# The two row-sum matmuls of the feed-forward input norm, set apart

## What is computed

```python
def rmsnorm(x, g):
    y = x * lax.rsqrt(jnp.mean(x * x, axis=-1, keepdims=True) + EPS)
    return y * g

def swiglu(h, w_gu, w_down):
    gate, up = jnp.split(h @ w_gu, 2, axis=-1)
    return (jax.nn.silu(gate) * up) @ w_down

x = x + swiglu(rmsnorm(x, norm_ffn[i]), ffn_w_gu[i], ffn_w_down[i])
```

## Time and profile before

| | us |
|---|---|
| median of 3 executions | 2921.4 (2918.1 to 2921.99) |
| the profiled execution | 2919.41 |
| its span, first to last instruction | 2917.4 |
| TensorE matmul records, busy | 2848.8 (98%) |
| TensorE weight loads, busy | 2798.8 (96%) |
| GpSimd busy | 2108.9 (72%) |
| ScalarE busy | 1325.1 (45%) |
| VectorE busy | 1074.1 (37%) |

### The profile page before, as it was taken

How to read it: one execution, slowest core, us unless ns; L and a number is a source line. 1 busy time by engine, 2 the same in 40 slices (tenths; PEclk the granted TensorE clock), 3 DMA queues, 4 the chain that set the end, 5 groups by cost and what they waited for, 6 DMA issues and landing times.

```text
span 2917.4 us, 55892 instructions
## 1 busy us (share of the span) xinstructions
PE 2848.8 (98%) x24180; PEld 2798.8 (96%) x24180; DVE 1074.1 (37%) x1883; ACT 1325.1 (45%) x1476; POOL 2108.9 (72%) x462
## 2 busy tenths in 40 slices
PE   8999999999999999999999999999999999999998
PEld 8999889999998899999999998999998999999998
DVE  4317444223165343245333135333134331353331
ACT  5344534344345454345443474543354433454432
POOL 6887558878876578876688783668786588666784
PEclk9999999999999899999999999999999999999999
DMA  8964335555554255554455542445554455544553
GB/s 229 209 209 154 136 124 185 188 186 193 197 180 146 105 201 183 184 180 145 145 188 188 188 175 73 156 163 188 188 189 159 146 187 188 175 155 148 183 185 109
DMA packets 74197, 496.88 MB, mean 170 GB/s; under 512 B 8399, under 2 KB 13135, under 8 KB 14968
## 3 DMA queue, kind: packets, MB, share of 16 engines
q1 hardware_dynamic: 68344, 485.88, 46.5%
q10 hardware_dynamic: 5632, 7.62, 2.5%
HBM read 490.05 MB, written 3.41 MB: 169 GB/s over the span
## 4 chain that ended last, share of the span: by engine, by line
PE 86%; POOL 3%; issue 3%; DVE 3%; DMA 3%; ACT 2%; SPq 0%; POOLq 0%; DVEq 0%; ACTq 0%
PE G L450 21%; PE G L451 21%; PE G L452 21%; PE S L450 6%; PE S L451 6%; PE S L452 6%; POOL wl L399 3%; DMA raw<-w_units 3%; PE G L656 1%; PE S L1006 1%; ACT wh L1077 1%; PE S L531 1%; PE S L805 0%; PE S L768 0%; PE S L762 0%
## 5 line engine op out<-in xcount | busy, mean ns | idle before, releaser
L399 POOL TENSOR_TENSOR wl<-raw,wh 128x2048 fp32r<-128x2048 f32 x458 | 2108.7, 4616 | 778.0 <-ACT wh L1077 757.0
L1077 ACT ACTIVATE wh<-raw 128x2048 fp32r<-128x2048 f32 x456 | 873.0, 1917 | 1086.5 <-DMA raw<-w_units 1086.3
L450 PE MATMUL G<-ah,wl 128*128 128x256 f32 x4304 | 1214.3, 282 | 12.0 <-DVE wl L1724 8.6
L451 PE MATMUL G<-al,wh 128*128 128x256 f32 x4304 | 1207.3, 281 | 0.0
L452 PE MATMUL G<-ah,wh 128*128 128x256 f32 x4304 | 1206.6, 280 | 0.0
L450 PEld LDWEIGHTS G<-ah,wl 128*128 128x128 f32 x4304 | 824.3, 192 | 20.1 <-issue 15.2
L452 PEld LDWEIGHTS G<-ah,wh 128*128 128x128 f32 x4304 | 815.9, 190 | 0.0
L451 PEld LDWEIGHTS G<-al,wh 128*128 128x128 f32 x4304 | 815.4, 189 | 0.4
L450 PE MATMUL S<-gh,wl 128*128 128x256 f32 x1408 | 395.0, 281 | 3.7 <-POOL wl L399 3.7
L451 PE MATMUL S<-gl,wh 128*128 128x256 f32 x1408 | 394.7, 280 | 0.0
L452 PE MATMUL S<-gh,wh 128*128 128x256 f32 x1408 | 394.6, 280 | 0.0
(11 more groups left out here) (367 smaller groups left out, 3787.5 us busy)
## 6 DMA issues: line engine op xcount, KB each, us to landing
raw<-w_units SPq DMA_DIRECT2D x459, 1024.0 KB, 4.8
bias<-tables ACTq DMA_DIRECT2D x24, 128.0 KB, 3.1
tables<-trow ACTq DMA_DIRECT2D x12, 192.0 KB, 9.1
con<-consts SPq DMA_DIRECT2D x1, 1056.0 KB, 16.9
x<-x_in SPq DMA_DIRECT2D x4, 256.0 KB, 5.6
raw<-w_units SPq DMA_DIRECT2D x4, 256.0 KB, 6.1
memx<-mem_in ACTq DMA_DIRECT2D x1, 1024.0 KB, 7.5
out<-full SPq DMA_DIRECT2D x4, 256.0 KB, 2.5
```

The costliest lines, as they stand in the source:

```text
L399: pool.tensor_tensor(wl[:, j * UW:(j + 1) * UW], raw[:, j * UW:(j + 1) * UW], wh[:, j * UW:(j + 1) * UW].bitcast(F32), ALU.subtract)\
L450: pe.matmul(out, sl, vh, start=start and k == 0, stop=False, **kw)
L451: pe.matmul(out, sh, vl, start=False, stop=False, **kw)
L1077: act.activation(wh[:, j * UW:(j + 1) * UW], raw[:, j * UW:(j + 1) * UW], ACT.Copy)\
```

## The change

In the feed-forward stages alone, the two matmuls of `row_sums` are issued in two places. A new function `row_sums_apart` takes the S bank ahead of unit 1 and returns a function `part(k)`: `part(0)` waits for `added` and issues the matmul on the first half of `full`, between the first and the second column half of unit 1; `part(1)` issues the matmul on the second half of `full` behind unit 1, and raises `sums_ready`. Mixers and cross-attention keep `row_sums`.

```diff
-            def features(out, j, xh, xl, fcs=2, col=256):
+            def features(out, j, xh, xl, fcs=2, col=256, halfway=None):
 
                 for fc in range(fcs):
+                    if fc and halfway is not None:
+                        halfway()
                     for k in range(KD):
...
+            def row_sums_apart():
+
+                out = s_bank(mean_used)
+
+                def part(k):
+                    if k == 0:
+                        pe.wait_ge(added, c.next(added))
+                    ins = pe.matmul(out[:, 0:T], ones[:, 0:P], full[:, k * T:(k + 1) * T], start=k == 0, stop=k == 1,
+                                    skip_group_check=True)
+                    if k:
+                        ins.then_inc(sums_ready, 1)
+                return part
...
+                    if u == 1:
+                        part = row_sums_apart()
                     if u == 0:
                         ins = features_by_input(G[g0 % 4], n0 % RING, ah, al, acts_ready, pieces=n == 0)
                     else:
-                        ins = features(G[(g0 + j) % 4], (n0 + j) % RING, ah, al)
+                        ins = features(G[(g0 + j) % 4], (n0 + j) % RING, ah, al,
+                                       halfway=(lambda: part(0)) if u == 1 else None)
                     ins.then_inc(unit_done, 1)
+                    if u == 1:
+                        part(1)
...
                     unit_of(u, u, n0 + u, free)
-                    if u == 1:
-                        row_sums(tokens=False)
```

## The result

The changed kernel takes 2897.6 us in the median of 8 executions (2882.9 to 2910.8) against 2921.1 us of the kernel before (8 executions, 2913.4 to 2926.8): a ratio of 0.9923, with a 95% interval of 0.9901 to 0.9946. It is faster by 23.5 us, where the prediction said 34. The profiled execution took 2891.9 us, its span is 2890.1 us.

The account below looks back on a forecast made before the run. TensorE bounds the kernel, by its number of matmuls times the distance between starts. Gains of 36.7 less 2.1 and 0.9 give 33.7 us, taking 2919.4 to 2885.7, as a median 2887 us; range 2879 to 2914.

Parts of the forecast that it names:

- the reading of two spacings: TensorE product stream: matmuls start 117.6 or 113.2 ns apart at the same clock, a remembered condition that row sums switch.
- The matmuls themselves, 0: Row sums on TensorE: splitting the two fp32 matmuls adds no fee, 0 us; upper bound 4 us.
- The wait, 0.9 us once: Third feed-forward stage: the first row-sum matmul, moved earlier, waits for VectorE's addition of squares, +0.9 us once.
- Two records should not arrive: short stays short: At a single row-sum matmul: two records are too few to drift to long; short stays short, long should leave short.
- its second leg: At the split row sums: if one matmul keeps or always turns the spacing, two give back the spacing from before unit 1.
- Sum over the feed-forward stages, 36.7 less 0.9: Feed-forward stretches behind the sums: all at short spacing gains 36.7 us, less 0.9 us of waiting.
- turned short by itself: First feed-forward stage, at 26.4 us: said to become short unaided 6 us later, leaving 0.2 us to gain.
- To give back: Stage beginning at 1672 us: entering its own row sums short, it leaves long, 475 matmuls x 4.4 ns, 2.1 us lost.
- mixed case: Feed-forward stages: phase, the half unit or the third stage's stall leaves some short, some long; half the gain, 2904 us; chance 0.16.
- Long everywhere: Feed-forward stages: one fp32 matmul leaves long spacing whatever came before; 2929 us, slower; chance 0.10.
- no tie: Feed-forward stages: spacing isn't tied to these interruptions, or stages drift back; only the wait remains, 2922 us; chance 0.08.
- the likeliest case: All eight feed-forward stages short behind their sums: 2887 us, own range 2880 to 2895; chance 0.66.

Follow-up runs that it names:

- second profile: The changed kernel, unaltered, run and profiled again: 2898.25 us, ratio 0.9941 to the kernel before.
- third profile: The changed kernel, unaltered, profiled once more in a single execution: 2899.35 us.
- more stages apart: Changed kernel with row sums half a unit later, plus the memory norm's last matmul and the recurrence's two sums set apart: 2897.98 us, ratio 0.9923.
- half a unit later: Changed kernel with the first row-sum matmul behind unit 1 and the second in the middle of unit 2: 2891.78 us, ratio 0.9913.
- three together: Kernel before with one useless fp32 matmul directly ahead of the two row sums in each feed-forward stage: 2893.07 us, ratio 0.9918; again 2890.65 us, 0.9892.

## Why the prediction came out as it did

The time was forecast at 2887 and is 2897.6; faster by 34 forecast, by 23.5 measured. By its steps:

**What bounds the kernel, and the reading of two spacings: right.** The large differences between the versions are those of the spacing behind their sums. No engine, queue or transfer took the gain back; the weights came at 193 to 196 GB/s through the long stretches at short spacing, and the earlier trace rows had 196.

**The matmuls themselves, 0: right.** Two records apart cost 0.43 us, four together 0.86.

**The wait, 0.9 us once: right.** From 640.79 to 641.78 is 0.99 us, less one step 0.88 us, ended by the addition at the line that the prediction named (1764, now 1782), and in no other stage.

**"Two records should not arrive: short stays short": wrong.** This was the mechanism proper. One matmul of 256 columns in full fp32, out of an undisturbed stream, turned the spacing in every one of the 105 places where the runs have one, 56 times to long and 49 times to short. The picture behind it, a full fp32 run that drifts towards leaving long from about its fourth record, is wrong too: three and seven matmuls, 6 and 14 records, leave short. What carried the forecast was its second leg, that two turns give the entering spacing back, with the same sum.

**Sum over the feed-forward stages, 36.7 less 0.9: right in the profiled execution,** 36.1 us there and 34.5 in the second profile (23.2 in the third, for the stall below). The windows that it was added up from reach into the next stage by up to 94 matmuls, 1.5 us of the gain together, so by stages it stood for some 34.3. One term was read wrongly. The first stage had not "turned short by itself": the two matmuls of the bias tables stand there, four records of another shape.

```profile
32.99 1.46 PE L1041 MATMUL S<-onehot,rel 33*12 33x384 f32 x4
```

Entered long, as in the kernel before, they left short in all five profiles where that was so; entered short, as in two of the three profiles of the change, they left short in three profiles and long in six. So this stage had a spacing to lose as well, and the forecast priced that at nothing. The windows of the changed kernel, and then of its third profile, behind these matmuls:

```profile
35.50:170.00 134.50, 134.50 (x1190) 1.00 0.89 209
```

```profile
35.60:170.00 134.40, 134.40 (x1144) 1.00 0.90 201
```

46 matmuls less in the same time are 5 us. The stage as a whole came out at -1.9, -0.5 and +1.6 us in the three profiles.

**"To give back", 2.1 us: mis-sized, since the clock had no term.** The stretch that it was about did turn as written (56.0 us for 478 matmuls). But mixers and cross-attention as a whole gave back 8.7, 3.5 and 3.1 us in the three profiles, where the forecast by stages comes to some 0.6 net. The difference is TensorE's granted clock. The windows of the first four-branch mixer, before and after, then a stall in it after the change and the stretch behind that stall:

```profile
203.80:451.20 247.40, 236.62 (x1872) 0.95 0.43 151
202.00:452.10 250.10, 238.88 (x1871) 0.94 0.42 150
...
432.81 0.39 PE L450 MATMUL G<-mh,wl 128*128 128x256 f32 x1 [2.44 <-DVE ml L2094]
...
433.10:436.40 3.30, 3.30 (x17) 0.50 0.00 0
```

Behind 2.4 us without work the clock is at 0.50, 1.2 GHz, for 3.4 us, and product matmuls start 213 ns apart instead of 113. In the profile of the kernel before TensorE stood idle there for 1.8 us, and the clock stayed at 1.00. Counted by distances of over 200 ns from start to start, 121 product matmuls in the mixers and cross-attention ran so before, and 206, 182 and 170 in the three profiles of the change. At 0.1 us each these are 8.5, 6.0 and 4.9 us more: about what was given back in the first profile, and more than that in the other two. So the two spacings by themselves gave back next to nothing between the stages. In the first stage the clock worked the other way, 44 such matmuls before and 28 after, 1.6 of its 1.9 us.

Whether the change itself makes the clock fall more often isn't shown. Over the whole span the granted clock is 0.986 in the mean of 69 executions of the kernel before, and 0.985 and 0.984 in the means of the two sets of the changed kernel, 8 and 7 executions. An estimate from these: 0.001 less clock over a span of 2900 us is 2.9 us, so this is some 3 to 6 us of the 10 or 11 by which the medians missed.

**The stall at the third stage priced as 0.9 us alone: too little.** The prediction named in its mixed case that it "may do the same to that stage", and gave it no term in the sum. It costs 0.9 us by itself, and in the one profile of three where it went wrong 11 us more (6.5, 1.7 and 2.8 us in the three stages told above), of which the stages of the first differential attention regained 3.1.

**The rest is the draw of the execution.** The execution profiled first lies 6 us below the median of its kernel, that of the earlier trace rows only 2 below its own; that is the way from 27.5 us to the 23.5 of the medians. How clock, stall and first stage share in the median is not shown. The scatter points at the wait as one part: the versions whose first part stands in the middle of unit 1 scatter over 19 to 28 us, the others over 8 to 15, and the kernel before over 10 to 19. But one version without the wait, that with more stages apart, scatters over 24; in its slowest execution the second to fourth stages came in long, behind 1.9 us without work in the first mixer.

**The rivals.** "Long everywhere" and "no tie" fell with the first windows. The Trainium skill ("TensorE: Matmul & The Clock Gate", "Back-to-back issue gap") gives the formula behind the 109.2 ns of the prediction for isolated warm matmuls, and says that in a stream of weight loads and matmuls both together set the spacing; it speaks of one spacing for a shape. By that none of these kernels could differ by more than its own added matmuls. The traces disagree: two matmuls together and the same two apart differ by 27 us on one chip, at granted clocks of 0.98 to 0.99 over the span in both. The measured time lies between the likeliest case and the mixed one, and that is also what happened: the stages short, with the third and the first left to chance, and a lower clock between them.

## What to carry to other kernels

When a kernel is bound by one engine and its instructions follow each other without a gap, divide the length of equal stretches by their count, stage by stage; a few per cent between equal stretches at the same clock is a finding, and the place where it begins names the cause. Then try the interruption in two or three forms, since its effect here went by its exact form and could not be derived: apart, one matmul more, half a unit later each cost a few lines. And price a new stall not only by its idle time: in this stream a stall can also bring out the worse spacing. The versions that take the same gain without the wait (first part behind unit 1, or three together) have ratios of 0.989 to 0.992, against 0.992 and 0.994 of the change; the intervals overlap, so they are the likelier choice and not a proven one. And read the granted clock of the stretches that the change doesn't touch, and profile a kernel more than once, before laying a few us to one stage: here the same stage of the same kernel differed by up to 6.5 us between profiles.

## What the runs showed of the hardware

- The product stream of this kernel has two spacings at a granted clock of 1.00, 113.3 and 117.8 ns from start to start of 256-column matmuls, and keeps one for over 1500 matmuls (1582 in 179.0 or 186.0 us). Which one, an interruption decides: 1 or 2 full fp32 matmuls of 256 columns turn it (the one alone in 105 of 105 places); 3 leave short from either side; 7 left short from either side; 8 leave long from either side, and 9 entered short left long. With the first of three 254 columns wide and two columns further on, the three turned it.
- The sums in the reduced format turned it in six of eight stages.
- Behind an idle time of 0.7 us the same single matmul left the spacing long for the half unit in two profiles; in a third it fell back to short by itself after seven matmuls.
- Four records of 384 columns on 33 partitions (the bias tables) left short when entered long, five times of five, and either spacing when entered short.
- Behind an idle time of 2.4 us in a mixer the granted clock was 0.50 (1.2 GHz) for 3.4 us, and products of 256 columns started 213 ns apart instead of 113; behind 1.8 us at the same place in the kernel before it stayed at 1.00.
- What in the engine remembers the spacing isn't shown. In a settled run of full fp32 the records start 216 ns apart with a 215 every sixth time, at its beginning mostly 215, and a narrower first matmul changes the outcome, so a few nanoseconds of phase between the fp32 run and the stream may decide; that is argued, not tested.
